# A hybrid encoder block on one core: branch A and the first chunk's output by seven products, that output behind the second chunk's branches, token sums on VectorE

## The reference

```python
h = rmsnorm(x, g_pre); proj = h @ w_in            # 1024 x 7440
(q_a, k_a, v_a, lr_a, z_a, q_b, k_b, v_b, z_b, m_a, m_b) = split_cols(proj)
o_a = rmsnorm(gla_mixer(q_a, k_a, v_a, log_a), g_gla) * silu(z_a)      # chunked linear attention
y_a = o_a @ w_branch_gla                                               # branch A, 1024 x 1024
o_b = swa_sink_mixer(rope(q_b), rope(k_b), v_b, sinks) * silu(z_b)     # window attention
y_b = o_b @ w_branch_swa                                               # branch B, 1024 x 1024
y = sigmoid(m_a + b) * y_a + sigmoid(m_b + b) * y_b
out = y @ w_out                                                        # 1024 x 1024
return x + rmsnorm(out, g_post)
```

## Time and profile before

| | us |
|---|---|
| median of 3 runs | 1955.2 |
| lowest, highest | 1953.82, 1959.33 |
| the profiled execution | 1951.45 |
| its span, first to last instruction | 1949.6 |
| TensorE busy in it | 1911.5 |
| GpSimd, VectorE, ScalarE busy | 987.4, 1239.7, 844.6 |
| TensorE's granted clock, share of full speed | 0.996 |

### The profile page before, as it was taken

One profiled execution on the slowest core, in us unless ns is written; L12 is line 12 of the kernel. 1 busy time (PEld: TensorE's weight loads), 2 busy tenths in 40 slices (PEclk: granted clock), 3 DMA queues, 4 the chain that ended last, 5 costly groups with the idle time before them and its releaser, 6 DMA issues. The chain is left out here.

```text
span 1949.6 us, 28906 instructions
## 1 busy us (share of the span) xinstructions
PE 1911.5 (98%) x9972; PEld 1533.0 (79%) x9972; DVE 1239.7 (64%) x2069; ACT 844.6 (43%) x1893; POOL 987.4 (51%) x667
## 2 busy tenths in 40 slices
PE   8999999999999999999999999999999999999996
PEld 7878877777777777888888787877777777788885
DVE  6868876977776667623154888768577675763104
ACT  5466474543444443324333664544433444432221
POOL 4643455555433357643563445557654333775444
PEclk9999999999999999999999999999999999999998
DMA  7524375667667677745433334457767666775612
GB/s 277 157 73 135 107 243 185 198 216 228 203 193 238 214 241 254 237 140 197 138 120 108 102 115 162 154 182 241 229 192 233 214 220 218 275 249 162 196 42 87
DMA packets 255140, 359.42 MB, mean 184 GB/s; under 512 B 31059, under 2 KB 156563, under 8 KB 242195
## 3 DMA queue, kind: packets, MB, share of 16 engines
q1 hardware_dynamic: 254995, 357.57, 56.9%
HBM read 237.50 MB, written 120.00 MB: 183 GB/s over the span
## 5 line engine op out<-in xcount | busy, mean ns | idle before, releaser
L878 PE MATMUL pu<-a_hi,w_hi 128*128 128x512 f32 x1740 | 688.8, 398 | 10.3 <-DVE u L1769 6.4
L878 PE MATMUL pu<-a_hi,w_lo 128*128 128x512 f32 x1740 | 674.6, 390 | 0.5 <-POOL w_lo L1888 0.5
L878 PE MATMUL pu<-a_lo,w_hi 128*128 128x512 f32 x1740 | 673.7, 390 | 0.0
L1888 POOL TENSOR_TENSOR w_lo<-t,w_hi 128x512 fp32r<-128x512 f32 x244 | 347.7, 1431 | 402.7 <-ACT w_hi L1222 402.6
L1888 POOL TENSOR_TENSOR w_lo<-w_raw,w_hi 128x512 fp32r<-128x512 f32 x267 | 378.9, 1429 | 254.5 <-ACT w_hi L1222 254.5
L878 PEld LDWEIGHTS pu<-a_hi,w_hi 128*128 128x128 f32 x1740 | 326.5, 188 | 94.2 <-issue 26.3
L878 PEld LDWEIGHTS pu<-a_hi,w_lo 128*128 128x128 f32 x1740 | 326.6, 188 | 70.6 <-POOL w_lo L1888 0.9
L878 PEld LDWEIGHTS pu<-a_lo,w_hi 128*128 128x128 f32 x1740 | 327.0, 188 | 63.6
L879 PE MATMUL pu<-a_hi,w_hi 128*128 128x512 f32 x640 | 249.2, 389 | 0.0
L879 PE MATMUL pu<-a_lo,w_hi 128*128 128x512 f32 x640 | 249.0, 389 | 0.0
L879 PE MATMUL pu<-a_hi,w_lo 128*128 128x512 f32 x640 | 249.0, 389 | 0.0
(11 more groups left out here) (183 smaller groups left out, 2476.3 us busy)
## 6 DMA issues: line engine op xcount, KB each, us to landing
w_raw<-in_w SPq DMA_DIRECT2D x81, 1024.0 KB, 7.0
va_d<-ct SPq DMA_DIRECT2D x32, 256.0 KB
qb_d<-ct SPq DMA_DIRECT2D x32, 256.0 KB
zb_d<-ct SPq DMA_DIRECT2D x32, 256.0 KB
q_s<-qb_d SPq DMA_DIRECT2D x32, 256.0 KB, 3.8
z_s<-zb_d SPq DMA_DIRECT2D x32, 256.0 KB, 3.1
gb_d<-gb SPq DMA_DIRECT2D x32, 256.0 KB, 3.6
za_d<-ct SPq DMA_DIRECT2D x32, 256.0 KB
```

Of the source, the lines that this page charges most:

```text
L878: return nc.tensor.matmul(dst, weights, moving, start=start, stop=stop, skip_group_check=True)
L1888: TT(flat(w_lo[o.n % NWB][:, :, :]), src, as_f32(flat(w_hi[o.n % NWB][:, :, :])), ALU.subtract) \
```

## The change

It does four things. (1) The groups run in another order: first chunk up to branch A, second chunk up to branch A, then the first chunk's output, then the second's. The merged y goes to DRAM (`y_d`) and comes back as fills. (2) yA 1 to 3 of both chunks and out 1 to 3 of the first chunk become fast; the second chunk's first "v" group becomes plain. So there are 69 fast and 13 plain groups, 587 products. Every phase now has the same table of fills, and its token places follow from those of the phase before (`next_slots`). (3) The sums S1 to S4 for branches B and A and for the first chunk's output are made by VectorE in `SUM_JOBS` and stored to DRAM; GpSimd makes the weight sums T3 and T1 for yA and yB. (4) The first chunk's norm (`NORM`, 16 pieces, now in seven buffers) moves into the second chunk's output phase, and its addition of x to VectorE.

```diff
-for _sb in range(NSB):
-    for _n, (_kind, _idx) in enumerate(ORDER):
-        _fast = (_n < NH and not (_sb == 0 and _n < PLAIN)) or (_kind == "yB" and _idx > 0)
+for _sb, _ws in ((0, range(NH + 8)), (1, range(NH + 8)), (0, range(NH + 8, NH + 12)), (1, range(NH + 8, NH + 12))):
+    for _w in _ws:
+        _kind, _idx = ORDER[_w]
+        _plain = _w in (0, NH, NH + 4, NH + 8) or (_sb == 0 and _w < PLAIN) or (_sb == 1 and _kind == "out")
...
+PHASES = ((0, "gb"), (0, "ga"), (1, "h"), (1, "gb"), (1, "ga"), (0, "y"), (1, "y"))
...
-for _sb in range(NSB):
-    _e = YBASE[_sb]
+for _sb, _what in PHASES:
+    _e = first_slot(_sb, dict(gb="yB", ga="yA", h="v", y="out")[_what])
     for _name, _load, _split, _free in (("A11", -10, -6, -7), ("A12", -9, -5, -6), ("A21", -5, -2, -5),
                                         ("A22", -4, -1, -4), ("S2", -1, 2, -3), ("S1", 0, 3, -2), ("S3", 3, 7, 6),
                                         ("S4", 4, 9, -1)):
-        fill(_sb, "gb", _name, GB_SLOT[_sb][_name], _e + _load, _e + _split, _e + _free)
-    for _name, _load, _split, _free in (("A11", 19, 23, 22), ("A12", 20, 24, 23), ("A21", 24, 27, 24),
-                                        ("A22", 25, 28, 25)):
-        fill(_sb, "ga", _name, GA_SLOT[_sb][_name], _e + _load, _e + _split, _e + _free)
...
+        if (_sb, _what) != PHASES[-1] or _name[0] == "A":
+            fill(_sb, _what, _name, SLOTS[_sb, _what][_name], _e + _load, _e + _split, _e + _free)
...
-NORM = {99 + 3 * x: x for x in range(16)}
-GPREP = {152 + 10 * j: j for j in range(KH)}
-NORM_BUFS = 3
+NORM = {9 + x: x for x in range(16)}
+for _sb in range(NSB):
+    _jobs = [("gb", BASE[0] + 152 + 10 * j, 0) for j in range(KH)]
+    if _sb:
+        _jobs = [("y", BASE[1] + 82 + 10 * j, 0) for j in range(KH)] + [("gb", BASE[1] + 150 + 10 * j, 0)
+                                                                        for j in range(KH)]
+    _jobs += [("ga", YBASE[_sb] + 4 + 6 * j, 1) for j in range(KH)]
...
+NORM_BUFS = 7
...
-def col_sums_on_vector(g):
-    return True
+def col_sum_on_vector(g, name):
+    return g.kind not in ("yA", "yB") or name in ("T2", "T4")
...
+            def load_sums(job):
...
+                sp.wait_ge(gs_out, 16 * 4 * job.n)
+                for q in range(4):
+                    e, t0 = 2 * job.j + q % 2, job.sb * SB + q // 2 * HT
+                    go(gx[job.place][q][:, :], rows_d[job.what][e * P:(e + 1) * P, t0:t0 + HT], gx_in)
...
-                        STT(tmp[c % 2][:, :], gate_a[c % 2][:, :], 1.0, bank[:, :], ALU.add, ALU.mult) \
-                            .then_inc(ya_ok, 1)
...
+                for k, tile_n in enumerate(TILE_ORDER):
+                    g = step(s, 4 + k)
+                    if g and g.kind == "out" and g.fast:
+                        act.wait_ge(c_ok[tile_n], fast_no(g) + 1)
+                        act.wait_ge(acc_ok, 4 * (g.idx - 1) + k + 1)
+                        A(tmp[k % 2][:, :], ct[tile_n][:, :], ACT.Square).then_inc(sq_out_ok, 1)
...
+                for k, n in enumerate(TILE_ORDER):
+                    g = step(s, 5 + k)
+                    if g and g.kind == "out" and g.fast:
+                        number = 4 * (g.idx - 1) + k
+                        pool.wait_ge(sq_out_ok, number + 1)
+                        pool.wait_ge(acc_ok, 2 + number)
+                        TT(acc[0][n // 2][:, :], acc[0][n // 2][:, :], tmp[k % 2][:, :], ALU.add).then_inc(acc_ok, 1)
```

482 lines of the change are left out of this document (250 added, 232 removed).

## The result

The changed kernel takes 2003.47 us (median of 4 runs, 2002.13 to 2005.98) where the kernel before takes 1954.51 (4 runs on the same chip): **ratio 1.0247, 95% interval 1.0227 to 1.0267**, slower. The forecast was 1940.0. What was to be saved was saved: the first page lines count 3 x 1964 + 3 x 384 = 7044 matmuls of 128x512, the predicted number. The span grew from 1949.6 to 2000.5 us all the same, so 50.9 + 21.8 = 72.7 us went elsewhere.

What follows compares the result with a forecast made beforehand. TensorE was taken to bound the kernel nearly everywhere. 1951.45 - 21.8 (products removed) + 6.6 (openings) = 1936.3; the same difference of -15.2 from the median 1955.2 gives 1940.0 us, range 1931 to 1949.

Steps and rivals of the forecast that it cites:

- What is removed: TensorE's queue: net 8 products of 595 go, leaving 7044 matmuls, at 2.72 us each: -21.8 us.
- Token sums for A: VectorE's added sum jobs: loads issued ahead, one to two products of slack, about 1 us for each of six jobs; priced at nothing.
- The openings: Phase starts with sums S1 to S4: three new ones at the mean of those seen, 2.2 us each: +6.6 us.
- so it fits: Branch A's fast groups on VectorE: 15 operations, 10 to 20 us per 19.0 us of TensorE, like branch B's; priced at nothing.
- The norm: First chunk's norm moved behind the second chunk's branches: at most 41 us of VectorE work in 43.5 us; priced at nothing.
- Rival 2: GpSimd becomes the bound, 93% busy in the first chunk's output; openings cost 4 to 5 us each: 1949 us; chance 0.19.
- GpSimd's T3 and T1: Weight sums of branches A and B moved to GpSimd: up to 3 us per B opening, VectorE relieved; taken as even.
- The first chunk's output by seven: First chunk's output phase: one of the three new openings with sums, priced at 2.2 us.
- The tail: From the final product to the end: keeps its form; growth beyond 23.7 us would show the prediction wrong.
- Rival 3: Transfers starve the A openings, needing 455 GB/s against 374 seen: 1962 us, slower than before; chance 0.07.

Runs made afterwards that it cites:

- the sums free: Changed kernel without branch A's sum jobs (its fills S1 to S4 read branch B's sums) and with the norm's sums five slots later: 1962.83 us.
- the holds: Kernel before with 14, 18, 22 and 26 additions in a row on VectorE ahead of four branch-A gates: 1981.05 us.

## Why the prediction was wrong

The chain of runs gives each term its size. From 2003.5: without A's jobs 1975.7; with the norm late 1962.8; with branch A plain 1955.3; the kernel before 1955.3 to 1956. The steps between single runs carry the differences said above, some us; by its own stage the norm's place cost 9.6 to 10.9 us (three pairs of runs) and not 12.9, and the jobs by the four branch stages 28.0.

| term | predicted | measured |
|---|---|---|
| branch A: six products fewer | -16.3 | -16.3 |
| branch A: the openings | +4.4 | +23.8 |
| branch A: its sum jobs on VectorE | 0 (up to 6) | +27.8 |
| norm in the last stage | 0 | +12.9 |
| rest: output by seven, `v` plain, B's sums, order | -3.2 | about 0 |
| together | -15.2 | +48 |

- **What is removed**: right, 8 products at 2.72 us, 7044 matmuls; between stops they are 0.2267 us apart as before.
- **Token sums for A: the step that failed first.** The text named the mechanism word for word: the load of a job waits for the stores of the one before, VectorE waits with it, and the bank additions stand behind. It then gave them "one to two products of slack" (2.7 to 5.4 us) and, with the cover gone, about 1 us for each job. The slack is smaller than such a block: four additions took 6.40 us at 743.53, 1.6 each, near the upper end of the 0.68 to 1.79 quoted, and the waits for the loads come on top. Eight jobs cost 27.8 us, 3.5 each; making the additions small gave back 7.8 of them, so the larger part is the jobs' waits for their loads and their transfers.
- **The openings**: 2.2 us each was read from phases whose fast groups have one gating to a tile. Branch A adds branch B's tile, four more VectorE operations with two SBUF inputs a group, and a second load a tile. Its openings cost 8.1 and 7.5 us with the sums free, and 4.7 and 3.9 more in the phases behind, which the prediction did not count at all; that the added operations are the reason fits, but is not shown. Two readings were wrong in "so it fits": a group of branch B had 13 such operations before (five additions, four gatings, four weight sums) and not 15, and its average of 57.7 of 81.4 us (branch A's is 71.6 of 90.8) hid the queue, in which a block in the wrong place stops TensorE.
- **The norm**: 0 was taken for its additions and transfers, which was nearly right (O2 at 90.7 with all of them in it is 3.7 us longer than before). The price was in the place of its first step, three products into the stage, while the squares were still being added. Rival 2 saw the engines of it, ScalarE's squares waiting for GpSimd's sums, and put it in the wrong stage.
- **The clock** was no term of the sum. Seven stops of 2.7 us or more stand between products in the changed kernel; the longest before was 2.3. In the four branch stages TensorE's waits are 36.1 us of 52.3 of excess; of the other 16.2, 13.7 are low clock behind six such stops, 1.8 to 2.7 for each by the starts of the matmuls, near what the holds showed.
- **GpSimd's T3 and T1**: taken as even, and even (2004.05 against 2003.5).
- **The first chunk's output by seven**: 2.2 forecast for its opening; 2.3 with branch A plain ahead of it, 6.2 to 7.3 behind branch A by seven.
- **The tail**: 23.7 forecast, 24.0 measured.
- **Rival 3** ended on the right side for the wrong reason. ScalarE waits 26.1 us for fills in A1's opening (13.7 for the sums, 12.4 for the quarters) and transfers touch 415 GB/s, but loading only a quarter of the sums' bytes shortens A1 by 2.2 us of its 11.9.

## What to carry to other kernels

Before a job is put into the queue of an engine that also frees another engine's buffers, read the gap between two of its freeing operations in that stretch and compare it with the job's whole block, its wait for data included, at the duration that such operations have there. An engine's average share says nothing on that. And when an idle time of TensorE is priced, add the low clock behind it: here 1.8 to 3.2 us for each stop of 2.7 us or more, and sometimes for one of 2.0 to 2.4. A phase that costs nothing only after a calm phase should be priced behind the phase that will really stand ahead of it.
